# First feed-forward of a block chain: six plain tile pairs beside sums of the normed input, then sixteen pairs by seven block products

## The reference, cut to what matters

```python
def swiglu(h, w1, w2):
    g, u = jnp.split(h @ w1, 2, axis=-1)
    return (jax.nn.silu(g) * u) @ w2

h_lat = h_lat + g2 * swiglu(modulate(rms_norm(h_lat, norm2_g[l]), sh2, sc2),
                            w_ffn_in[l], w_ffn_out[l])
```

## Time and profile before

| | us |
|---|---|
| median of 3 runs | 3389.88 |
| lowest, highest | 3387.67, 3390.45 |
| the profiled execution | 3392.9 |
| its span | 3391.1 |
| mean granted clock of TensorE | 0.99 |

### The profile page before, as it was taken

The page is one execution under the profiler, slowest core; times in us unless marked ns, Lnnn a source line. Parts: engine busy times, 40 slices in busy tenths (PEclk is TensorE's granted clock), DMA queues, the critical chain, the costliest instruction groups (busy, mean ns, idle before and its releaser), DMA issues.

```text
span 3391.1 us, 47136 instructions
## 1 busy us (share of the span) xinstructions
PE 3309.1 (98%) x18750; PEld 2794.0 (82%) x18750; DVE 1872.6 (55%) x3335; ACT 1416.2 (42%) x2517; POOL 1680.6 (50%) x996
## 2 busy tenths in 40 slices
PE   8999999999999999999999999999999989999998
PEld 5767788887888898988777999899987769998776
DVE  4266775433222386842667576557624667682655
ACT  4533323423322353533445354444434455352643
POOL 4323445554544455655525565565646346564432
PEclk9999999999999999999999999999999999999999
DMA  7212334442344423234312323332343113233221
GB/s 285 69 51 63 95 98 131 148 143 75 123 154 137 151 94 100 100 104 116 85 35 89 102 100 105 95 112 88 107 109 111 32 60 116 96 109 99 73 63 56
DMA packets 102218, 345.95 MB, mean 102 GB/s; under 512 B 12174, under 2 KB 12558, under 8 KB 101839
## 3 DMA queue, kind: packets, MB, share of 16 engines
q1 hardware_dynamic: 101200, 341.10, 31.4%
q10 hardware_dynamic: 798, 1.85, 0.2%
HBM read 336.08 MB, written 2.10 MB: 100 GB/s over the span
## 4 chain that ended last, share of the span: by engine, by line
PE 88%; DVE 5%; ACT 3%; POOL 1%; DMA 1%; issue 1%; SPq 0%; DVEq 0%; ACTq 0%
PE ps L1477 17%; PE ps L1479 16%; PE ps L1478 16%; PE ps L1513 8%; PE ps L1514 8%; PE ps L1515 8%; PE ps L1540 2%; PE ps L1541 2%; PE ps L1542 2%; PE ps L1827 2%; PE ps L1854 1%; PE ps L1837 1%; ACT t L1929 1%; PE ps L1746 1%; POOL t L3179 1%
## 5 line engine op out<-in xcount | busy, mean ns | idle before, releaser
L3179 POOL TENSOR_TENSOR t<-t,t 128x1024 fp32r<-128x1024 f32 (+2 forms) x408 | 923.2, 2269 | 1162.2 <-ACT t L1914 1153.0
L1477 PE MATMUL ps<-t,t 128*128 128x512 f32 x2608 | 1046.2, 401 | 11.6 <-POOL t L3179 5.9
L1479 PE MATMUL ps<-t,t 128*128 128x512 f32 x2608 | 1026.1, 393 | 0.0
L1478 PE MATMUL ps<-t,t 128*128 128x512 f32 x2608 | 1025.1, 393 | 0.0
L3189 POOL TENSOR_TENSOR t<-t,t 128x512 fp32r<-128x512 f32 x440 | 572.2, 1329 | 361.7 <-ACT t L1929 361.7
L1513 PE MATMUL ps<-t,t 128*128 128x256 f32 x2464 | 695.7, 282 | 18.4 <-POOL t L3189 7.1
L1514 PE MATMUL ps<-t,t 128*128 128x256 f32 x2464 | 694.9, 282 | 0.0
L1515 PE MATMUL ps<-t,t 128*128 128x256 f32 x2464 | 693.7, 282 | 0.0
L1477 PEld LDWEIGHTS ps<-t,t 128*128 128x128 f32 x2608 | 493.1, 189 | 140.7 <-issue 23.9
L1479 PEld LDWEIGHTS ps<-t,t 128*128 128x128 f32 x2608 | 492.3, 189 | 110.3
L1478 PEld LDWEIGHTS ps<-t,t 128*128 128x128 f32 x2608 | 493.1, 189 | 103.8 <-issue 1.7
(11 more groups left out here) (325 smaller groups left out, 3613.3 us busy)
## 6 DMA issues: line engine op xcount, KB each, us to landing
t<-in_w_f1i SPq DMA_DIRECT2D x88, 512.0 KB, 3.8
t<-in_w_f2i SPq DMA_DIRECT2D x88, 512.0 KB, 3.7
t<-in_w_ada SPq DMA_DIRECT2D x72, 512.0 KB, 4.3
t<-in_w_ffi SPq DMA_DIRECT2D x44, 512.0 KB, 3.7
t<-in_w_f1o SPq DMA_DIRECT2D x32, 512.0 KB, 4.0
t<-in_w_f2o SPq DMA_DIRECT2D x32, 512.0 KB, 4.1
t<-in_w_gate SPq DMA_DIRECT2D x24, 512.0 KB, 4.2
t<-in_w_out SPq DMA_DIRECT2D x48, 256.0 KB, 2.6
```

Source lines behind the costliest of these rows:

```text
L1477: e.matmul(out, wh[:, at], X.hi[c][:, 0:N], start=c == first, stop=False)
L1478: e.matmul(out, wh[:, at], X.lo[c][:, 0:N], start=False, stop=False)
L1479: m = e.matmul(out, wl[:, at], X.hi[c][:, 0:N], start=False, stop=c == final)
L3179: e.tensor_tensor(k.WL[k.slot[n]][:, 0:w], k.raw[:, j % NRAW, 0:w], f(k.WH[k.slot[n]][:, 0:w]), ALU.subtract).then_inc(*k.rest.inc(('rest' ...
```

## The change

The first six tile pairs stay plain. Beside tiles 1 to 4 the sums t1 to t4 of the normed input are made (`turn_even` behind the gate, `turn_odd` behind the up): per tile five copies on ACT and ten operations on DVE, in two PSUM banks G and H. Tiles 6 to 13 and 14 to 21 are then made by the seven products, by the routine that the four later feed-forwards use. The weight operands of pair 6 are begun between the steps of plain tile 5, those of pair 14 in the last two `e` tiles. Side steps: two after each of the six plain tiles, none in the pairs, three after each of the first six `e` tiles and two after the other two, one after each of the first four `d` tiles: again 38. The rotation of the rounded weight slots over four places instead of three starts at tile 6 and no longer behind the feed-forward. The ring for the gate's result has three buffers instead of four.

```diff
-PARTS, PAIRS = (((0, 14), (14, 8)), ((0, 8), (8, 14)))
+PARTS, PAIRS, PLAIN = (((0, 14), (14, 8)), ((0, 8), (8, 14)), 6)
...
-        (plain if m.scale is None else fours)(on, m, first, count)
-        after = (m.next, 0) if part else (None if m.scale is None else m, first + count)
+        if first < m.start:
+            plain(on, m)
+            on.rotate(8, 0)
+        fours(on, m, max(first, m.start), first + count - max(first, m.start))
+        after = (m.next, 0) if part else (m, first + count)
         for n in range(KT):
             on.T(('ed'[part], m.tag, n), m.wo, n, m.mid, kt=count, first=first)
-            for _ in range(n < 4 if part else 2):
+            for _ in range(n < 4 if part else 3 if n < 6 else 2):
                 next(m.side, None)
...
-def plain(on, m, first, count):
-    for i in range(first, first + count):
+def plain(on, m):
+    for i in range(m.start):
...
         on.ffn_gate(m, i)
+        if 0 < i < 5:
+            on.turn_even(m, i - 1)
+        if i == m.start - 1:
+            begin_pair(on, m, m.start, KT - 2)
         if i:
             on.T(('u', m.tag, i), m.wi, FF + i, m.A)
         on.ffn_up(m, i)
-        if i > 2:
+        if 0 < i < 5:
+            on.turn_odd(m, i - 1)
+        if i == m.start - 1:
+            begin_pair(on, m, m.start, KT - 1)
+        for _ in range(2):
             next(m.side, None)
...
+    def turn_even(self, m, j):
...
+        e.copy(pairs(b), f(k.HH)[:, 2 * j:2 * j + 2, 256:512]).then_inc(*k.act.inc(('turn high', j)))
...
+        self.wait_ge('turned', j, 't1')
+        e.copy(T.hi(j, 't1'), b[:, 0:256]).then_inc(*k.act.inc(('hi', A.tag, j, 't1')))
+
+    def turn_odd(self, m, j):
...
+        self.wait_ge('turned', j, 't4')
+        e.copy(T.hi(j, 't2', 2), b).then_inc(*k.act.inc(('hi', A.tag, j, 't2')))
+        e.copy(T.hi(j, 't4'), c[:, 0:256]).then_inc(*k.act.inc(('hi', A.tag, j, 't4')))
```

More of the change, by code:

```diff
@@ L635, in first @@
         norm(on, m, j)
-    twin = short(banked(Sum('f1_0', k.R[0], S, ('normed', 'n2', 7), range(8), 0, [('lo', ('mid', 'ff1'), FF - 1)])))
-    first = banked(Sum('fin1', k.R[1], S, ('normed', 'cn', 7), range(8)))
+    twin = short(banked(Sum('f1_0', k.R[0], S, ('filled', ('u', 'ff1', FF - 1)), range(8), 0, [('lo', ('mid', 'ff1'), FF - 1)])))
+    first = banked(Sum('fin1', k.R[1], S, ('filled', ('u', 'ff1', FF - 1)), range(8)))
     first.slots = twin.slots
@@ L1280, in block, with pairs @@
     return k.raw[:, j % NRAW, :].rearrange('p (c t n) -> p t c n', t=2, n=128)[:, int(piece[2]) - 1]
+def pairs(ap):
+    return ap.rearrange('p (a n) -> p a n', a=2)
 def four(ap):
@@ L1511, in product @@
             at = slice(128 * j, 128 * j + 128)
[L1512 to L1515, removed]
+            self.wait_ge(*m.sums.ready(j, x))
+            e.matmul(out, wh[:, at], m.sums.hi(j, x), start=opens and j == 0, stop=False, skip_group_check=not opens)
+            e.matmul(out, wh[:, at], m.sums.lo(j, x), start=False, stop=False, skip_group_check=not opens)
+            mm = e.matmul(out, wl[:, at], m.sums.hi(j, x), start=False, stop=j == 3, skip_group_check=not opens)
         if js[-1] == 3:
@@ L1940, in pair_gate @@
     def pair_gate(self, m, i):
-        self.ffn_gate(m, i)
+        k, e = (self.k, self.e)
+        if m.scale is not None:
+            self.ffn_gate(m, i)
+            return
+        b = self.take(m.ring(k), 'm', m.tag, i)
+        self.wait_ge('last sum', m.tag, i)
+        e.activation(b, self.bank('A', m.tag, i), ACT.Silu).then_inc(*k.act.inc(('silu', m.tag, i), ('free', ('A', m.tag, i))))
     def pair_up(self, m, i):
@@ L2836, in mixture, with turn_even, turn_odd @@
             self.low(A, j, self.k.O[:, j, :])
+    def turn_even(self, m, j):
+        k, e, A, T, b = (self.k, self.e, m.A, m.sums, self.bank('G', m.tag, j))
+        self.wait_ge('turn high', j)
+        e.tensor_tensor(b, b, f(A.hi[2 * j]), ALU.subtract).then_inc(*k.dve.inc())
+        self.settle()
+        e.tensor_tensor(pairs(b), pairs(b), f(k.HL)[:, 2 * j:2 * j + 2, 256:512], ALU.add).then_inc(*k.dve.inc())
+        self.settle()
+        e.tensor_tensor(b, b, f(A.lo[2 * j]), ALU.subtract).then_inc(*k.dve.inc(('turned', j, 't1')))
+    def turn_odd(self, m, j):
+        k, e, A, T, b, c = (self.k, self.e, m.A, m.sums, self.bank('G', m.tag, j), self.bank('H', m.tag, j))
+        one, three, hi, lo = (b[:, 0:256], c[:, 0:256], f(A.hi[2 * j + 1]), f(A.lo[2 * j + 1]))
+        self.wait_ge('hi', A.tag, j, 't1')
+        e.tensor_tensor(T.lo(j, 't1'), one, f(T.hi(j, 't1')), ALU.subtract).then_inc(*k.dve.inc(('lo', A.tag, j, 't1')))
+        self.settle()
+        e.tensor_tensor(one, hi[:, 256:512], one, ALU.subtract).then_inc(*k.dve.inc())
+        self.settle()
+        e.tensor_tensor(one, lo[:, 256:512], one, ALU.add).then_inc(*k.dve.inc())
+        self.settle()
+        self.lent('H', m.tag, j)
+        e.tensor_tensor(three, hi[:, 0:256], one, ALU.subtract).then_inc(*k.dve.inc())
+        self.settle()
+        e.tensor_tensor(three, lo[:, 0:256], three, ALU.add).then_inc(*k.dve.inc(('turned', j, 't4')))
+        self.wait_ge('hi', A.tag, j, 't2')
+        e.tensor_tensor(T.lo(j, 't2', 2), b, f(T.hi(j, 't2', 2)), ALU.subtract).then_inc(*k.dve.inc(('lo', A.tag, j, 't2'), ('lo', A.tag, j, 't3'), ('free', ('G', m.tag, j))))
+        self.wait_ge('hi', A.tag, j, 't4')
+        e.tensor_tensor(T.lo(j, 't4'), three, f(T.hi(j, 't4')), ALU.subtract).then_inc(*k.dve.inc(('lo', A.tag, j, 't4'), ('free', ('H', m.tag, j))))
     def sum_parts(self, res, n):
```

54 lines of the change are left out of this document (47 added, 7 removed).

## The result

| | before | after |
|---|---|---|
| median us | 3390.16 | 3412.74 |
| lowest, highest | 3387.67, 3395.19 | 3411.12, 3419.85 |
| profiled execution, its span | 3392.9, 3391.1 | 3412.38, 3410.6 |

The ratio is 1.0065, with a 95% interval from 1.0052 to 1.0077: the change costs 22.6 us, and at least 17. The direction was forecast, the size was not: 8.8 us against 22.6, just outside the range of 3383 to 3411.

The account below looks back on a forecast made before the run. It took TensorE, busy 98% of the span, as the bound: matmul time and gaps. Terms -15.7 + 9.65 + 1.7 + 12.15 + 1.2 - 0.7 + 0.5 = +8.8 us on 3389.9 gave 3398.7, range 3383 to 3411.

Parts of the forecast that it names:

- Ring and turn work: Plain tiles and switch: loads of g3 and pair 6 wait five places behind side steps that follow turn work.
- the first knot: Plain tiles: gaps of 2.9 us before g2 and 6.7 before g3, +9.65, plus +1.7 for low clock behind g3's gap.
- the walk: Step-by-step timing of loads and queues through plain tiles and switch, from times of before; gave the gaps, +9.65 and +12.15 us.
- that rule for S1: Switch to pair 6: DVE and GpSimd locking each other out would make the knot an estimated 1.3 us longer for two sums.
- The closing of the side group: Side group closed in tile 3: its work moves but is not more; no term in the sum.
- Second knot: Switch to pair 6: late raw tiles and DVE queue delay p1, p6 and p3, +12.15 us, plus +1.2 for the clock.
- Gain: 16 pairs by seven products: pitch from 10.88 to 9.90 us each, -15.7 us.
- Clock behind the forecast gaps: Slow matmuls after long gaps: +1.7 us behind g3, absorbed behind g2, +1.2 at the switch.
- Small terms: Gap at entry of `e` goes, -0.7 us; entering pairs from `e`, +0.5; three side loads per `e` tile, 0 and up to +3.
- B: Rival: neither knot comes, only a 2.05 us gap at the switch with its clock; 3377.2 us, chance 0.13.
- C: Rival: only one knot comes; 3387.3 us without the first, 3388.6 without most of the second; chance 0.25.
- D: Rival: DVE's backlog at the switch is not paid back in pair 7; 3410.9 us and more, chance 0.07.

Follow-up runs that it names:

- x1: Changed kernel with none of the twelve side steps in the six plain tiles; one each behind pairs 7 to 12 and 14 to 19; ratio to before 1.0046.
- x2: Changed kernel without side steps in plain tiles 4 and 5; those four follow pairs 14 to 17; ratio to before 1.0060.
- x3: Changed kernel without side steps in plain tiles 0 to 3; those eight follow pairs 8, 9 and 14 to 19; ratio to before 1.0068.
- x4: Changed kernel with one side step ahead of gate and one ahead of up in tiles 1 to 5, two behind pairs 14 and 15; 3411.15 us, ratio 1.0052.
- x7: Changed kernel with one side step per plain tile, three per `e` tile, one per each of eight `d` tiles; ratio to before 1.0010.
- x10: x7 with the rotation of the four rounded weight slots started at the fourth slot, which no plain tile uses; ratio to before 1.0005.
- x11: x12 with the plain tiles' product of gate and up in PSUM, as in x5; ratio to before 0.9984.
- x12: x10 with two side steps instead of three in the last two `e` tiles, two instead of one in the first two `d` tiles; ratio to before 1.0004.
- x13: x11 without the side step behind plain tile 4; a third `d` tile has two steps for it; ratio to before 0.9993.
- x5: Changed kernel with the plain tiles' product of gate and up written into the up tile's PSUM bank; ratio to before 1.0051.
- x6: Changed kernel with one side step per plain tile, four behind the first four `e` tiles, three behind the others, one behind the first four `d` tiles; ratio to before 1.0038.

## Why the prediction was right in kind and wrong in size

**Ring and turn work: right, and shown.** The forecast said that g3 and pair 6 would come late because their loads stand five places behind side steps that stand behind turn work. Both gaps had their place and releaser, 3.24 and 6.08 against 2.9 and 6.7 forecast, and x1 to x3 removed each with its side steps alone; at the switch 2.14 us before p1 stayed, where the forecast has 2.05.

**The step that failed first: the first knot, +11.35 forecast, some 16.9 measured** (18.7 of tiles 0 to 5 less 1.8 for the closing that moved). Three terms of the walk were mis-sized.

The low part of product 1 was taken at 0.69, from the row of before, where GpSimd was at rest. In the changed kernel it began 0.5 us behind a GpSimd operation and took 2.44; tiles 2 to 4 have 2.47, 2.44 and 1.87. Each of the four ends 0.55 to 0.56 us after the GpSimd operation beside it. This step stands ahead of a4 and a5, so g3's load went out at 873.50 + 1.24 = 874.7 in the times of before, where I had 873.2. The Trainium skill, "SBUF — State Buffer", section "🔬 SBUF: two separate sides", says that a VectorE operation with two SBUF inputs and a GpSimd one shut each other out for a whole instruction. The trace agrees with it at this operation, 2.44 against 0.69 out of PSUM. I had weighed that rule for S1 at the switch and dropped it. There it bears on one of two sums: S1 of pair 6 took 0.70 with GpSimd at rest, S1 of pair 7 took 1.59 beside it, and neither the 1.34 of the walk.

The load was taken at 3.70. That load of before had two others behind it within 0.9 us, and none ahead of it for 15 us. SP and ScalarE of the changed kernel:

```profile
872.11 0.33 SPq L1389 DMA_DIRECT2D t<-in_w_ada  x1
873.50 1.28 SPq L1389 DMA_DIRECT2D t<-in_w_ffi  x3
...
878.47 1.04 ACT L1970 CAST t<-t 128x1024 fp32r<-128x1024 f32 x1 [8.36 <-DMA t<-in_w_ffi]
```

Two side sums in a row let go of two loads, 1.39 us apart: the side load that follows a4's sum, then g3 behind a5's. So g3 is sent while a load ahead of it is still under way, and it took 4.97. The profiles read for this agree: weight loads that had none ahead of them for over 3 us took 3.5 to 4.2 us to their first reader, with two more behind them or not (before, x1, x4, x7, x10 to x13); those 1.39 behind a side load took 4.1 to 6.2 (the changed kernel, x2, x5). No run varies this alone. Together PE began g3 at 883.3 in the times of before, 2.9 later than forecast.

The closing of the side group was said to move only. It now waited 0.98 for the late side sum [<-DVE t L2628 above], and behind it the granted clock was at its lower level for some 3 us, about 1.6 lost. That had no term in the sum. The two side sums ahead of it took 4.61 us, where the walk has 2.66 for two, with a GpSimd operation beside them. Their rows, and the window behind the closing:

```profile
890.85 4.61 DVE L2628 SCALAR_TENSOR_TENSOR t<-t,t,t 128x1024 f32<-128x1024 f32 x2
...
891.17 3.20 POOL L3291 TENSOR_TENSOR t<-t,t 128x1024 fp32r<-128x1024 f32 x1 [4.65 <-ACT t L1970]
```

```profile
899.00:901.00 2.00, 2.00 (x6) 1.57 (x5) 1.56 (x1) 0.40 (x1) 2.00 (x1) 0.50 1.03 406
```

g3's 2.9 and the closing's 0.98 and 1.6 are 5.5 us, which is what 16.9 has over 11.35.

**Second knot, +13.35 forecast, 15.2 measured** (95.4 less 79.2 for eight pairs at 9.90, less 1.0 of pitch, below). p3 began 22.4 us behind the end of u5 (920.9); the walk had 20.65. The load of pair 6's first raw tile went out 1.5 us ahead of that end, where the walk has 2.55, and took 4.1 instead of 3.7, so p1 began at 4.7 and not at 3.2. The second raw tile was there for S1 only at 4.9, where I had 2.45:

```profile
919.40 0.33 SPq L1389 DMA_DIRECT2D t<-in_w_ffi  x1
...
923.54 0.62 ACT L1985 CAST t<-t 128x512 fp32r<-128x512 f32 x1 [6.50 <-DMA t<-in_w_ffi]
...
925.84 0.70 DVE L2512 TENSOR_TENSOR ps<-t 128x512 f32<-128x512 f32 x1 [6.47 <-DMA t<-in_w_ffi]
```

**Gain, -15.7 forecast, -13.6 measured.** Two silus of the new pairs:

```profile
976.91 0.60 ACT L2005 ACTIVATE t<-ps 128x512 f32<-128x512 f32 x1 [0.51 <-DVE ps L2557]
...
986.94 0.60 ACT L2005 ACTIVATE t<-ps 128x512 f32<-128x512 f32 x1 [0.51 <-DVE ps L2557]
```

The pitch is 10.03 and not 9.90, 119.4 ns a matmul against 117.9, without a gap and with the clock at 1.00. The undisturbed pairs of this feed-forward have 9.98 to 10.06 in the changed kernel, x2, x4, x5, x7 and x10 to x13; over 16 pairs that is 16 x 0.13 = 2.1 us. Its cause stays open. Twelve matmuls take 1.42 to 1.44 us whatever their input is; in `f1_0`, 1.41 to 1.42.

**Clock behind the forecast gaps: right.** Windows of 2 us behind g2's gap, behind g3's and behind p3's (columns as the earlier trace rows):

```profile
866.00:868.00 2.00, 2.00 (x6) 1.61 (x5) 1.93 (x4) 0.00 (x0) 0.47 (x1) 0.50 0.00 0
886.00:888.00 2.00, 2.00 (x11) 1.65 (x10) 1.93 (x4) 0.00 (x0) 0.52 (x1) 1.00 0.00 0
944.00:946.00 2.00, 2.00 (x12) 2.00 (x11) 0.00 (x0) 0.43 (x1) 2.00 (x2) 0.50 0.03 8
```

Behind g2's gap PE was slow for some 6 us, behind g3's for 3, and the first cost nothing, since g3 hung on VectorE, as forecast.

**Small terms: right in sum, one by luck.** 0.4 at pair 14 (0.5 forecast), three side steps per `e` tile at no cost: `e` has 1.1 more with 1.8 of closing in it, which leaves the -0.7. But the gap of the earlier trace rows at 1002.84 stands ahead of the second `e` tile and not at the entry of `e`, which is at 992.4. It went, and another of 0.48 came ahead of the last `e` tile, so the gaps by themselves give only 0.2 less. x6 and x13 show that the room in `e` was near the edge.

**Rivals.** B and C are out: neither knot failed to come. D is out: pair 7 follows pair 6 at 10.2 and later pairs at 10.0. The sum of the measured terms is -13.6 + 16.9 + 15.2 - 0.7 + 0.4 = +18.2, and 18.1 is seen. So of the 13.8 us between forecast and result, 5.5 are the first knot, 1.9 the second and 2.1 the pitch. Some 4.5 are no term of the walk: 22.6 in the medians against 18.1 in the stages, and no run puts them down to the change.

## What to carry to other kernels

Where several streams share one ring of buffers in program order, a load waits for whatever stands a ring's length ahead. So before work is added to an engine, look which ring entries its queue releases, and count the places to the loads that must not be late. Price a wait with the duration that the neighbours allow at the new place and not with the one of a quiet row; and when a wait is removed, compute what is late next: here the 1.5 us that x10 took off one wait came back in the next.

## What the runs showed of the hardware that I had not expected

- A VectorE low part with both inputs in SBUF took 2.44 us beside a GpSimd operation (the changed kernel) and 0.69 with one input in PSUM (x5_psum). The side sum, 1.28 in a quiet stretch, took 2.36 beside GpSimd in x1_none.
- A 512 KB load with none ahead of it for over 3 us took 3.5 to 4.2 us from issue to its first reader, also with two more issued within 0.9 us behind it; issued 1.39 us behind another it took 4.1 to 6.2. The same load in the same order took 4.97 us in the changed kernel, 6.12 in x5_psum and 6.17 in x2_first.
- The same 84 matmuls of 256 columns took 10.03 us in one feed-forward and 9.90 in another, both without gaps and at full granted clock.
